# Two-layer encoder step: latent projections moved among the index scores, gate projections moved behind them and into the attention, latent products in rounded parts, first output product moved forward

## What is computed

```python
h = rmsnorm(x, g_norm) * (1 + scale[:, None]) + shift[:, None]
z = h @ w_in
cq, ckv, kr, ga, qb, kb, vb, qi, ki, wi, gb, ma, mb = jnp.split(z, split_idx, axis=-1)
q = (rmsnorm(cq, g_qnorm) @ w_uq)              # latent queries, 384 -> 8 heads x 96
ckv = rmsnorm(ckv, g_kvnorm)                   # latent keys/values, 256 wide
kn, va = mla_expand(ckv, w_ukv)
oa = mla_attend(...)                           # dense attention
idx_score = jnp.einsum('bqh,bqhs->bqs', wi, jax.nn.relu(score))
vals, idx = lax.top_k(idx_score, topk)         # 128 (prompt), 136 (sample) keys a query
ob = dsa_attend(...)                           # sparse attention over those keys
ya = (oa * jax.nn.silu(ga)) @ w_oa
yb = (ob * jax.nn.silu(gb)) @ w_ob
m = jax.nn.sigmoid(ma) * ya + jax.nn.sigmoid(mb) * yb
x = x + gate[:, None] * (m @ w_out)
```

## Time and profile before

| | us |
|---|---|
| median of 3 runs | 1138.65 |
| lowest and highest run | 1137.5 and 1140.14 |
| the profiled execution | 1136.84 |
| its span in the profile | 1135.0 |
| PE busy | 1070.3 |
| DVE, ACT, POOL busy | 732.3, 474.9, 349.6 |
| granted clock of PE, mean over the span | 0.972 |

### The profile page before, as it was taken

One profiled execution on the slowest core, in us unless ns is written; L12 is line 12 of the kernel. 1 busy time (PEld: TensorE's weight loads), 2 busy tenths in 40 slices (PEclk: granted clock), 3 DMA queues, 4 the chain that ended last, 5 costly groups with the idle time before them and its releaser, 6 DMA issues.

```text
span 1135.0 us, 19935 instructions
## 1 busy us (share of the span) xinstructions
PE 1070.3 (94%) x7724; PEld 931.0 (82%) x7724; DVE 732.3 (65%) x1510; ACT 474.9 (42%) x1068; POOL 349.6 (31%) x208
## 2 busy tenths in 40 slices
PE   6999999999999999899989999999999999989995
PEld 3797986878788888799969789587887888879994
DVE  4538997646786777555672799955476323874655
ACT  4536455433444434414253554543354443451322
POOL 1346450220122222333334553302121222333340
PEclk9899999899999999899999999999899999999997
DMA  9581221201144445224314112121112121441322
GB/s 363 204 259 41 75 72 61 76 19 57 38 139 144 135 146 168 75 85 180 134 58 147 70 59 78 60 75 38 38 38 70 57 85 41 145 131 57 138 91 79
DMA packets 33774, 114.27 MB, mean 101 GB/s; under 512 B 4616, under 2 KB 5352, under 8 KB 31760
## 3 DMA queue, kind: packets, MB, share of 16 engines
q1 hardware_dynamic: 32352, 110.47, 29.2%
q10 hardware_dynamic: 1328, 2.53, 0.6%
HBM read 105.86 MB, written 7.12 MB: 100 GB/s over the span
## 4 chain that ended last, share of the span: by engine, by line
PE 82%; DVE 6%; ACT 5%; issue 3%; POOL 2%; DMA 2%; SPq 1%; POOLq 0%; DVEq 0%; ACTq 0%
PE pj L715 19%; PE pj L717 18%; PE pj L716 18%; PE ps L933 4%; PE po L1007 4%; PE turned L976 3%; PE pj L881 2%; PE ps L946 2%; DMA wide<-in_ada 2%; DVE squares L1587 1%; PE pj L855 1%; PE po L993 1%; POOL w_lo L1696 1%; PE pj L866 1%; PE ps L796 1%
## 5 line engine op out<-in xcount | busy, mean ns | idle before, releaser
L715 PE MATMUL pj<-h_hi,w_hi 128*128 128x272 f32 x1776 | 530.7, 299 | 17.4 <-POOL h_lo L1755 10.4
L717 PE MATMUL pj<-h_lo,w_hi 128*128 128x272 f32 x1776 | 518.0, 292 | 0.0
L716 PE MATMUL pj<-h_hi,w_lo 128*128 128x272 f32 x1776 | 515.7, 290 | 0.0
L1696 POOL TENSOR_TENSOR w_lo<-ring,w_hi 128x1024 fp32r<-128x1024 f32 x112 | 271.5, 2424 | 582.6 <-ACT w_hi L1095 582.6
L715 PEld LDWEIGHTS pj<-h_hi,w_hi 128*128 128x128 f32 x1776 | 339.6, 191 | 38.0 <-issue 28.3
L716 PEld LDWEIGHTS pj<-h_hi,w_lo 128*128 128x128 f32 x1776 | 340.1, 191 | 0.2
L717 PEld LDWEIGHTS pj<-h_lo,w_hi 128*128 128x128 f32 x1776 | 338.9, 191 | 0.0
L1095 ACT ACTIVATE w_hi<-ring 128x1024 fp32r<-128x1024 f32 x112 | 118.9, 1062 | 155.0 <-PE pj L717 139.0
L1587 DVE CUSTOM_DVE_ANT_0 squares<-ring,silu_c 128x1024 f32<-128x1024 f32 x64 | 84.6, 1322 | 1.4
L1544 DVE TENSOR_SCALAR probs<-probs,inv 128x128 f32<-128x128 f32 (+4 forms) x136 | 80.7, 593 | 4.8
L1318 ACT ACTIVATE wide<-pj 128x272 f32<-128x272 f32 x64 | 25.4, 397 | 114.5 <-PE pj L717 114.2
(11 more groups left out here) (285 smaller groups left out, 1342.1 us busy)
## 6 DMA issues: line engine op xcount, KB each, us to landing
ring<-in_wts SPq DMA_DIRECT2D x150, 512.0 KB, 3.5
wide<-in_xT SPq DMA_DIRECT2D x4, 1088.0 KB, 5.7
wide<-in_ada SPq DMA_DIRECT2D x3, 1024.0 KB, 20.2
ring<-in_wts SPq DMA_DIRECT2D x6, 384.0 KB, 3.1
x_between<-wide ACTq DMA_DIRECT2D x8, 272.0 KB, 2.0
wide<-x_between SPq DMA_DIRECT2D x2, 1088.0 KB, 6.3
bias_p<-in_ada SPq DMA_DIRECT2D x2, 1024.0 KB, 8.9
bias_p<-bias_rows SPq DMA_DIRECT2D x1, 2048.0 KB, 11.8
```

What stands on the lines that cost most here:

```text
L715: pe.matmul(out, hi, h_hi[:, k, half(b)], start=(k == first), stop=False)
L716: pe.matmul(out, lo, h_hi[:, k, half(b)], start=False, stop=False)
L717: return pe.matmul(out, hi, h_lo[:, k, half(b)], start=False, stop=(k == stop))
L1696: pool.tensor_tensor(w_lo[:, slot, :], ring[:, ring_slot[splits[n]], :], w_hi[:, slot, :].bitcast(F32), ALU.subtract).then_inc(s_wlo, 1)
```

## The change

Six things change, in both layers.

- Among the index scores stand the ten projections of `ckv` and `cq`; the eight of `ga` follow them. POOL adds the squares in three steps, so that four matmuls instead of ten sum them.
- `uk`, `uv` and `uq` join `SPLIT`: their products become three rounded ones each (48 of 128x512 and 108 of 128x272), with five more tiles to round.
- All four tiles of `gb` become fillers of the attention: 18 fillers instead of 14 in the units 0 to 16. Unit 0 has two, the units 1 to 16 one each, where 5, 10 and 15 had none.
- The selection of block 3 moves from ahead of the attention into the units 1 to 6 (3, 3, 3, 3, 2 and 2 rounds), and that of block 4 into the units 7 to 23.
- The latents are normed after block 1's selection, and DVE forms their low parts (`latents_lo`).
- At the end of the attention, the outputs of the first half are split earlier, `ya` (0, 0) stands ahead of the last values, and the low parts of the second half of `gate_a` are made by DVE in place of POOL.

The core of the diff:

```diff
-SPLIT = ("kx", "qi", "vb", "ga", "ckv", "cq", "gb", "qb", "kb", "ma", "mb", "wo", "wx")
+SPLIT = ("kx", "qi", "vb", "ga", "ckv", "cq", "gb", "qb", "kb", "ma", "mb", "wo", "wx",
+         "uk", "uv", "uq")
...
-    t += [("ga", n, P, 1024) for n in range(4)] + [("ckv", n, P, 1024) for n in range(2)]
-    t += [("cq", n, P, 1024) for n in range(3)] + [("gb", n, P, 1024) for n in range(4)]
+    t += [("ckv", n, P, 1024) for n in range(2)] + [("cq", n, P, 1024) for n in range(3)]
+    t += [("ga", n, P, 1024) for n in range(4)]
     t += [("uk", 0, P, 1024), ("uv", 0, P, 1024)] + [("uq", n, P, 768) for n in range(3)]
-    t += [("ukt", n, 64, 1024) for n in range(2)]
+    t += [("ukt", n, 64, 1024) for n in range(2)] + [("gb", n, P, 1024) for n in range(2)]
...
-        u = FIRST_DSA + (i - dense) * FIRST_DSA // 31 if i >= dense else i * (FIRST_DSA - 2) // (dense - 1)
+        u = FIRST_DSA + (i - dense) * (FIRST_DSA - 1) // 31 if i >= dense else i * (FIRST_DSA - 2) // (dense - 1)
...
-    f = [("gb", t, b) for t in range(EARLY_GB, 4) for b in range(2)]
+    f = [("gb", t, b) for t in range(4) for b in range(2)]
...
-    after = [("ga", t, b) for t in range(4) for b in range(2)] + [("ckv", 0, b) for b in range(2)]
+    after = [(k, t, b) for k, n in (("ckv", 2), ("cq", 3)) for t in range(n) for b in range(2)]
...
+        widx = {1: gate_b[:, 1, 0:256], 2: gate_b[:, 0, 0:384], 3: qb[:, 3, 0:TP]}
...
+        lat_hi = [latents_a[:, n, :] for n in range(5)]
+        lat_lo = [latents_b[:, n, :] for n in range(2)] + [latents_c[:, n, :] for n in range(3)]
+        lat_sq = [gate_a[:, 3, :], qb[:, 2, :], gate_a[:, 0, :], gate_a[:, 1, :], gate_a[:, 2, :]]
...
-                for kind, n in (("ckv", 2), ("cq", 3)):
-                    for t in range(n):
-                        for b in range(2):
-                            if (kind, t) != ("ckv", 0):
-                                project((kind, t, b))
-                pe.wait_ge(s_irl, len(isteps))
-                for n in range(5):
-                    pe.wait_ge(s_lsq, past(s_lsq) + n + 1)
+                for t in range(4):
                     for b in range(2):
-                        out = ps[:, b, 0:HF] if n < 2 else pt[b][:, 0:HF]
-                        last = pe.matmul(out, ones[:, :], squares[:, n % 3, half(b)],
-                                         start=(n in (0, 2)), stop=(n in (1, 4)))
-                    last.then_inc(s_lst, 1)
-                for t in range(EARLY_GB):
-                    for b in range(2):
-                        project(("gb", t, b))
-                pe.wait_ge(s_lno, 1)
-                loaded("uk", 0)
...
+                        project(("ga", t, b))
+                        if (t, b) == (0, 0):
+                            latent_sum(0, 1, lat_sq[0])
+                            pe.wait_ge(s_vb, 2)
+                            latent_sum(1, 3, lat_sq[2])
+                def query(job, tile, a, b):
+                    out = bank(job)
+                    for c in range(3):
+                        hi, lo = part_of(w_hi, tile)[:, 3 * a + c, :], part_of(w_lo, tile)[:, 3 * a + c, :]
+                        pe.matmul(out[:, 0:HF], hi, lat_hi[2 + c][:, half(b)], start=(c == 0), stop=False)
+                        pe.matmul(out[:, 0:HF], lo, lat_hi[2 + c][:, half(b)], start=False, stop=False)
+                        last = pe.matmul(out[:, 0:HF], hi, lat_lo[2 + c][:, half(b)], start=False, stop=(c == 2))
+                    last.then_inc(s_full, 1)
+                pe.wait_ge(s_llo, past(s_llo) + 1)
+                pe.wait_ge(s_wlo, split_no["uk", 0] + 1)
...
-                        last = pe.matmul(out[:, 0:TP], wt[:, c, P * t:P * t + P], ckv[:, c, 0:TP],
-                                         start=(c == 0), stop=(c == 1))
+                        hi, lo = part_of(w_hi, ("uk", 0))[:, 4 * c + t, :], part_of(w_lo, ("uk", 0))[:, 4 * c + t, :]
+                        pe.matmul(out[:, 0:TP], hi, lat_hi[c][:, 0:TP], start=(c == 0), stop=False)
+                        pe.matmul(out[:, 0:TP], lo, lat_hi[c][:, 0:TP], start=False, stop=False)
+                        last = pe.matmul(out[:, 0:TP], hi, lat_lo[c][:, 0:TP], start=False, stop=(c == 1))
...
+                def attended(kind, f, b):
+                    a = int(kind == "yb")
+                    out = bank((kind, f, b))
+                    for t in range(4):
+                        if f == 0:
+                            pe.wait_ge(s_gblo if a else s_galo, 4 * b + t + 1)
+                        last = three(out[:, 0:HF], ("wo", f), 4 * a + t, b, 4 * a, 4 * a + 3)
+                    last.then_inc(s_full, 1)
...
+                    if u == NU:
+                        pe.wait_ge(s_wlo, split_no["wo", 0] + 1)
+                        attended("ya", 0, 0)
...
+                    n = job[1] + 2 * (job[0] == "cq")
+                    latent_out(n, job[2])
+                    if job[2]:
+                        act.activation(lat_sq[n], (ckv if n < 2 else cq)[:, job[1], :], ACT.Square).then_inc(s_lsq, 1)
+                        prepare()
...
+                latent_root(0, KVL)
+                latent_root(1, QL)
+                for t in range(4):
+                    for b in range(2):
+                        gate(("ga", t, b))
                     prepare()
...
-                for t in range(EARLY_GB):
-                    for b in range(2):
-                        gate(("gb", t, b))
-                    prepare()
-                for h in range(NH):
-                    last = act.activation(k_mla[64:96, h, :], kr[64:96, 0:TP], ACT.Copy)
-                last.then_inc(s_kr8, 1)
+                    if t < 2:
+                        for h in range(4 * t, 4 * t + 4):
+                            last = act.activation(k_mla[64:96, h, :], kr[64:96, 0:TP], ACT.Copy)
...
+                            act.wait_ge(s_lno, 1)
+                            latents_hi(0, 2, ckv)
+                    elif t == 2:
+                        act.wait_ge(s_lno, 2)
+                        latents_hi(2, 3, cq)
...
-                    if job[2]:
+                    if job[2] and job != ("mb", 7, 1):
...
+                    if u == NU:
+                        output_hi(gate_a, 0, range(2), 1, s_gahi)
...
-                    if u == NU:
+                    if u == NU - 1:
...
-                output_hi(gate_a, 0, range(4), 1, s_gahi)
+                output_hi(gate_a, 0, range(2, 4), 1, s_gahi)
+                prepare()
...
-                select(2, TOPK_P // 8)
-                select(3, 6, end=False)
...
+                def latents_normed(first, count, latent, gain, n):
+                    dve.wait_ge(s_lrt, past(s_lrt) + n + 1)
+                    link(dve.reciprocal(rstd[n], rstd[n]))
+                    for c in range(count):
+                        last = dve.scalar_tensor_tensor(out=latent[:, c, :], in0=latent[:, c, :], scalar=gain[:, layer, c:c + 1],
+                                                        in1=rstd[n], op0=ALU.mult, op1=ALU.mult)
+                    last.then_inc(s_lno, 1)
+                def latents_lo(first, count, latent, n):
+                    dve.wait_ge(s_lhi, past(s_lhi) + n + 1)
+                    for c in range(count):
+                        last = dve.tensor_tensor(lat_lo[first + c], latent[:, c, :], lat_hi[first + c].bitcast(F32), ALU.subtract)
+                    last.then_inc(s_llo, 1)
+                latents_normed(0, 2, ckv, g_kv, 0)
+                latents_normed(2, 3, cq, g_q, 1)
+                select(2, 2, end=False)
+                latents_lo(0, 2, ckv, 0)
+                latents_lo(2, 3, cq, 1)
+                select(2, TOPK_P // 8 - 2)
...
+                        output_lo(gate_a, 0, range(4), 1, s_gahi, s_galo)
+                    if u == NU - 1:
                         output_lo(gate_a, 0, range(4), 0, s_gahi, s_galo)
                         output_lo(gate_b, 4, range(3), 0, s_gbhi, s_gblo)
-                    if 1 <= u < 1 + TOPK_S // 8:
-                        select(4, 1, end=(u == TOPK_S // 8))
+                    if 1 <= u <= 6:
+                        select(3, 3 if u <= 4 else 2, end=(u == 6))
+                    if 7 <= u < 7 + TOPK_S // 8:
+                        select(4, 1, end=(u == 6 + TOPK_S // 8))
...
+                adds = {1: (0, 1), 3: (2, 3), 4: (2, 4)}
+                for i in range(5):
+                    if i in adds:
+                        a, b = adds[i]
+                        pool.wait_ge(s_lsq, past(s_lsq) + i + 1)
+                        if i == 4:
+                            pool.wait_ge(s_lsa, past(s_lsa) + 2)
+                        pool.tensor_tensor(lat_sq[a], lat_sq[a], lat_sq[b], ALU.add).then_inc(s_lsa, 1)
+                    rest()
...
+                pool.wait_ge(s_sel, 2)
+                for t in range(4):
...
-                for t in range(4):
-                    pool.wait_ge(s_gahi, 4 + t + 1)
```

(18 more changed lines are left out.)

138 lines of the change are left out of this document (56 added, 82 removed).

## The result

The changed kernel takes 1121.02 us in the median (1120.68 to 1121.85, 4 runs) against 1138.97 before (1137.5 to 1140.14, 4 runs): a ratio of 0.9851, 95% interval 0.9838 to 0.9863. It is 18 us faster; 34 were forecast, and the time lies 1 us above the range. The profiled execution took 1121.35 us, its span is 1119.6, 15.4 less than before's.

What follows compares the result with a forecast made beforehand. PE's own work and its few idle stretches were taken to set the time. Layer 0 at -17.0 and layer 1 at -17.2 made -34.2 us, so 1104.4 us from the median 1138.65, with a range of 1088 to 1120.

Steps and rivals of the forecast that it cites:

- the second half: Attention's later units: a wait at unit 21 goes, block 4's rounds cost 0.5 us; layer 0 -1.1, layer 1 -2.0.
- term 7: Units 1 to 6: three selection rounds for one on DVE delay PE, +2.0 us per layer (0 to +6).
- terms 4 and 5: Latents stage, per layer: earlier norming removes idle time, -2.7 us; lateness from five more tiles on POOL adds +2.0.
- Terms 1 and 2: Latents' products, per layer: rounded matmuls replace float32 ones, -2.8 us for uk and uv, -2.9 for the queries.
- term 3: Sums of squares, per layer: ten matmuls become four, -2.75 us.
- Term 6: Units 5, 10 and 15: new fillers cover PE's waits for ACT's copies, -4.1 us per layer (-2 to -4.5).
- POOL holds DVE up: Rival: seven more POOL tiles beside waiting DVE work cost +5.6 us per layer, giving 1115.6; chance 0.04.
- what would prove the sum wrong: Anywhere in the kernel: the clock falling where it was full, which no part of the sum included; no size given.
- Layer 1's slow stretch: Layer 1 attention, from 791.30: 12.70 us at clock 0.60 cost 5.1 us; half was counted as gained through a filler.
- End of the attention: Last stretch of each attention: POOL's low parts no longer awaited, 1.8 us stays idle; layer 0 -4.7 us, layer 1 -4.0.
- the port rule: End of the attention: DVE and GpSimd lock shared ports, so DVE's h_lo waits for POOL's w_lo; -2.3 us instead of -4.7.
- Slower than before: Rival: PE waits for DVE in units 1 to 8 keep the clock at 0.60, +30 us per layer, 1165; chance 0.04.

Runs made afterwards that it cites:

- experiment 7: The changed kernel with the products of uk, uv and uq in float32 again, without the five extra tiles and the query latents' low parts: 1129.52 us.
- experiment 2: The kernel before with block 4's 17 selection rounds in the units 1 to 6 instead of one in each of units 1 to 17: 1140.36 us, ratio 1.0013.
- experiment 4: The changed kernel with block 4's 17 selection rounds in the units 7 to 17, none in the units 18 to 23: 1118.99 us.
- experiment 8: The kernel before with only the change's new end of the attention: 1132.6 us, ratio 0.994.

## Why the prediction was wrong

The direction and the products were right; 16.6 us of gain were missing between the medians, 18.9 by the stretches of the two traces. Of the 18.9, 10.5 lie in the two attentions (terms 6 and 7 and the second half; term 7 alone misses 6.2, 10.2 us in the units 2 and 3 against 4.0), 5.7 in the stages from the first index score to unit 0 (terms 1 to 5: -6.9 and -5.8 where -9.2 was forecast for each), 4.0 at the two ends of the attention, and the 1.3 that were gained ahead of the first index score go off. So the first step that failed is term 7, what three rounds a unit on DVE cost PE, then terms 4 and 5, the idle time ahead of the latents' products, and then what stays idle at the end of the attention.

- **Terms 1 and 2, products.** The stretches above give 5.97 + 5.66 = 11.6 us for 48 matmuls of 128x512, 0.242 each with the change of banks, where 0.227 was taken: -2.1, not -2.8. The 54 of the queries take 6.77, 0.125 each, as read: -2.9. Together 10.0 us in both layers; experiment 7 measured 8.5, net of the tiles.
- **Terms 4 and 5, idle time of the latents stage: mis-sized.** 2.7 us were to go and 2.0 to come. In layer 0 the three waits at 138.15, 145.00 and 152.33 are 2.9 us, in layer 1 the one at 694.66 is 2.35, with a slow stretch behind it. The idle time was replaced, not shortened: with the products as measured and term 3 as read, -6.9 and -5.8 leave +0.9 and +2.0 us for the two terms, where -0.7 was forecast. I compared POOL's 2.4 us for a tile with PE's 6.1 and named the gates without adding them up. Four gate steps of 0.77 and a tile of 2.39 are 5.5 us and would still have fitted; what I didn't see is that they stretch to 6.9 beside DVE's norming and low parts, which the change puts at the same place.
- **Term 6 was right.** The units 5, 10 and 15 gave -1.9, -1.2 and -1.2 us in layer 0, 4.3 against 4.1. In layer 1 the units 10 and 15 gave -1.2 each.
- **Term 7 failed, in the step "I take +2.0".** That is what the rounds cost alone (experiment 2: 0.43 + 1.57). The units 2 and 3 cost 5.9 and 4.3 us, because a `w_lo` of POOL fell on DVE's scaling in unit 1, in front of the rounds (1.9 us lost, as in the earlier trace rows, where it was 1.6), and the longer wait was followed by a stretch at half clock. Both mechanisms stood in the text, the one as the rival "POOL holds DVE up" at 0.04, the other as what would prove the sum wrong; I priced each by itself and not where they meet. A like combination, a held scaling, one round and the modulation tiles, made unit 24 of layer 0 longer by 3.9 us, of which experiment 4 gives 2.1 to the round; the gain of 1.6 came, in unit 22, and I had 0.5 for the rounds.
- **Layer 1's slow stretch** at 791.30 went as a whole (-6.5 in the units 5 and 6, of it some 1.9 for the wait), more than the half that I counted; a new one in the units 7 and 8 took 3.2 back. That the filler removed it is not shown: it is missing in experiments 2 and 8 too, where the wait ahead of it stands as before (1.59 and 1.58 us).
- **End of the attention: too high, because too little was left standing.** -4.7 and -4.0 were forecast, -2.3 and -2.4 came (-2.7 in experiment 8). I took 1.8 us as what stays idle. No wait for POOL's low parts is left, but PE waits 0.86, 0.44, 1.79 and 1.11 us for ACT and DVE, 4.2 against 5.4 before. The low clock behind the old wait, which cost some 2.5 us, is gone in this trace. I weighed the port rule against the change and set it aside without a row that spoke against it, and it held: POOL's tile starts 0.05 us ahead of DVE's third low part of `gate_a`, which takes 2.60 us and ends 0.3 us behind the tile, while the other three take 0.43 or 0.44. In layer 1 it is the same, 2.61. The longest of PE's waits stands behind it. Four low parts away from a tile, four beside it, the tile, and the wait:

```profile
458.79 1.50 DVE L1619 TENSOR_TENSOR h_lo<-gate_a,h_hi 128x272 fp32r<-128x272 f32 x4
...
463.79 3.67 DVE L1619 TENSOR_TENSOR h_lo<-gate_a,h_hi 128x272 fp32r<-128x272 f32 x4
...
464.45 2.35 POOL L1725 TENSOR_TENSOR w_lo<-ring,w_hi 128x1024 fp32r<-128x1024 f32 x1 [12.21 <-ACT w_hi L1109]
```
```profile
467.16 0.39 PE L726 MATMUL pj<-h_hi,w_hi 128*128 128x272 f32 x1 [1.79 <-DVE h_lo L1619]
```

  The value worked out by the rule, -2.3, is what came in both layers. (The time given beside it, 1109.2, should have been 1108.5, since layer 1 had -4.0 in the sum.)
- **Slower than before** did not happen: the slow stretches of the attention lasted 3 to 10 us each, not 45.

## What to carry to other kernels

When work is moved onto an engine with little idle time, lay its new list against the idle times unit by unit, and put the work where the gaps are; the same 16 rounds took 12 us more in one order than in another, by the medians. Price two delays of one engine together if they can fall into the same unit: here the held scaling alone cost nothing and the rounds alone 2 us a layer, both together 5.9 and 4.3. And count what an engine does between two deliveries, gates and all and at the lengths that they have beside their neighbours, against the time in which they are used up.
